# Sparse expert weights by indexed accumulating DMAs instead of one-hot products; expert tiles turned two ahead

## The reference, cut to what matters

```python
def block(xb):                                   # 128 tokens
    q = (xb @ w_q).reshape(t, 8, 2, 128)
    s = einsum('thpd,hpkd->thpk', q, sub_keys)   # 8 heads, 2 key sets of 128
    sv, si = top_k(s, 16)
    cand = sv[:, :, 0, :, None] + sv[:, :, 1, None, :]
    cv, ci = top_k(cand.reshape(t, 8, 256), 16)  # 16 experts of 16384 for each token and head
    idx = i1 * 128 + i2;  g = softmax(cv)
    act = gelu(einsum('thkd,td->thk', expert_down[idx], xb))
    return einsum('thk,thkd->td', g * act, expert_up[idx])
```

## Time and profile before

| | |
|---|---|
| median of 3 runs | 4651.68 us (4647.34 to 4653.0) |
| the profiled execution | 4650.75 us |
| its span, first to last instruction | 4649.0 us |
| mean granted TensorE clock | 0.969 |
| busy: TensorE matmul / VectorE / ScalarE / GpSimd | 92% / 56% / 29% / 31% |
| moved by DMA | 838.99 MB, 180 GB/s mean |
| `queries` | about 1600 to 1876 us |
| `experts_down` | 1876 to 3385 us |
| `experts_up` | 3385 us to the end |

### The profile page before, as it was taken

One profiled execution on the slowest core, in us unless ns is written; L12 is line 12 of the kernel. 1 busy time (PEld: TensorE's weight loads), 2 busy tenths in 40 slices (PEclk: granted clock), 3 DMA queues, 4 the chain that ended last, 5 costly groups with the idle time before them and its releaser, 6 DMA issues. The chain is left out here.

```text
span 4649.0 us, 69126 instructions
## 1 busy us (share of the span) xinstructions
PE 4286.5 (92%) x22902; PEld 3639.0 (78%) x22933; DVE 2599.5 (56%) x5422; ACT 1341.0 (29%) x2021; POOL 1432.2 (31%) x1022
## 2 busy tenths in 40 slices
PE   8999999897997799799999999999979999999998
PEld 3788877686776689798999999999957777777776
DVE  3555211255665333677889898897644444444444
ACT  1132433344222421233333333333221111111112
POOL 0333333354334021222111111111144444444442
PEclk9999999899998899899999999999989999999999
DMA  7222233344562422555566665666587777777776
GB/s 272 56 95 95 99 104 98 93 118 118 165 195 90 152 64 63 177 198 197 173 215 218 204 207 198 219 215 210 199 270 245 248 246 249 246 250 248 251 248 213
DMA packets 632585, 838.99 MB, mean 180 GB/s; under 512 B 227732, under 2 KB 448164, under 8 KB 632484
## 3 DMA queue, kind: packets, MB, share of 16 engines
q1 hardware_dynamic: 514468, 476.96, 32.5%
q0 software_dynamic: 73728, 268.47, 17.3%
q10 hardware_dynamic: 44288, 92.29, 5.1%
HBM read 674.03 MB, written 163.58 MB: 180 GB/s over the span
## 5 line engine op out<-in xcount | busy, mean ns | idle before, releaser
L1874 PE MATMUL p_u<-h2T_hi,downT_hi 128*128 128x384 f32 x2048 | 715.0, 349 | 103.4 <-DVE downT_lo L1979 85.3
L1874 PE MATMUL p_u<-h2T_hi,downT_lo 128*128 128x384 f32 x2048 | 693.9, 339 | 0.0
L1874 PE MATMUL p_u<-h2T_lo,downT_hi 128*128 128x384 f32 x2048 | 692.8, 338 | 0.0
L1852 POOL DMA_INDIRECT down_rows<-in_peer_down_dram,row_ids x256 | 262.4, 1025 | 1264.4 <-DVE row_dots L2002 1187.8
L2381 PE MATMUL p_y<-up_hi,coef_hi 128*128 128x512 f32 x1488 | 587.2, 395 | 0.0
L2381 PE MATMUL p_y<-up_lo,coef_hi 128*128 128x512 f32 x1488 | 580.4, 390 | 0.0
L2381 PE MATMUL p_y<-up_hi,coef_lo 128*128 128x512 f32 x1488 | 579.4, 389 | 0.0
L2282 DVE TENSOR_TENSOR y_acc<-p_y,y_acc 128x512 f32<-128x512 f32 x372 | 256.4, 690 | 540.5 <-PE p_y L2381 540.5
L1874 PEld LDWEIGHTS p_u<-h2T_hi,downT_hi 128*128 128x128 f32 x2048 | 391.3, 191 | 116.4 <-issue 116.4
L2178 POOL TENSOR_TENSOR up_lo<-up_raw,up_hi 128x1024 fp32r<-128x1024 f32 x128 | 323.0, 2524 | 419.8 <-ACT up_hi L2212 418.7
L508 PE MATMUL p<-hT_hi,w_hi 128*128 128x512 f32 x1024 | 405.0, 396 | 0.0
(11 more groups left out here) (343 smaller groups left out, 7888.8 us busy)
## 6 DMA issues: line engine op xcount, KB each, us to landing
down_raw<-in_peer_down_dram SPq DMA_DIRECT2D x128, 512.0 KB, 4.4
up_raw<-in_peer_up_dram SPq DMA_DIRECT2D x128, 512.0 KB, 5.3
scratch_gu<-gelu_out ACTq DMA_DIRECT2D x128, 384.0 KB, 2.3
gelu_in<-scratch_gu SPq DMA_DIRECT2D x128, 384.0 KB, 4.1
weights_in<-scratch_w SPq DMA_DIRECT2D x128, 384.0 KB, 6.4
w_raw<-in_w_in_dram SPq DMA_DIRECT2D x64, 512.0 KB, 4.0
w_ada_sb<-in_w_ada_dram SPq DMA_DIRECT2D x12, 2048.0 KB, 15.4
scratch_w<-weights_out SPq DMA_DIRECT2D x48, 512.0 KB, 3.7
```

Of the source, the lines that this page charges most:

```text
L1852: pool.indirect_dma_start(out=rows[:, n % ROWS, :], out_offset=None, in_=inp["peer_down"][0], in_offset=bass.IndirectOffsetOnAxis(ap=row_i ...
L1874: mm = pe.matmul(ps_u[u][half][:, 0:HD], d[:, u, k, :], h2[h][:, k, half * HD:(half + 1) * HD], start=(n == 0), stop=(n == 3 * KD - 1))
```

## The change

Four things, all for the expert layer.

1. The weight matrix is not built from one-hot products any more. `scratch_w` is now `[128 expert tiles, 128, 768 tokens]` and is set to zero during `project_in`, with 64 DMAs of two expert tiles each from a zeroed SBUF tile. Then, for each head of a dense block, the 16 picks of 128 tokens are sent with 16 indirect DMAs that add (`compute_op=ALU.add`): each writes 128 single floats, one for a token, at the offset expert x 768 + token, which VectorE makes as `sent_ids`. A head's sends wait until the last send of the head before has landed. Five heads of the first dense block are selected and sent in `queries`, the other 43 in `experts_down`. The one-hot operations on VectorE, their products on TensorE, ScalarE's copies and SP's stores of weights are gone.
2. `experts_down` has 51 selections (8 for fetched block 1, 43 dense), spread over the first 60 of 64 steps by `head_of`, the fetched ones taking turns with the first dense ones. Row gathers have a ring of 14 buffers and are issued two steps ahead; dot products go straight to `row_u`.
3. Expert tiles are turned two ahead: two PSUM buffers `p5_down`, four buffers each of `down_raw`, `downT_hi`, `downT_lo` and `gelu_out`.
4. `experts_up` reads `weights_in` in runs of 3072 bytes and waits for no weight store; `row_spread` has four buffers and is made a group ahead; the quads stand after slots 4 and 8, and two of them in the first group, after which the other groups have one pair each. Most hardware loops are written out.

The core of the diff:

```diff
+SENT = 4
+EARLY = 5
+RING = 14
...
# project_in, SP
                         sp.dma_start(w_raw[:, u], w_in(col, i)).then_inc(w_loaded[u], 16)
+                        if isinstance(i, int) and i == 0:
+                            sp.wait_ge(zero_set, 1)
+                        sp.dma_start(scratch["w"][bass.ds(i * CLEAR, CLEAR)].rearrange("e p t -> p e t"),
+                                     zero[:].unsqueeze(1).to_broadcast([P, CLEAR, TD])).then_inc(w_cleared, 16)
...
+def select_end(dve, b, step, exp_done, n, id_f, ids, scale, weight, chosen):
+    dve.wait_ge(step, n * SEL_STEPS + 24)
+    dve.scalar_tensor_tensor(id_f, b["pick"][:, 0], float(PK), b["pick"][:, 1], ALU.mult, ALU.add).then_inc(step, 1)
     dve.wait_ge(exp_done, n + 1)
     dve.reciprocal(b["inv"][:], b["exp_sum"][:]).then_inc(step, 1)
...
+        dve.tensor_scalar(ids, id_f, float(TD), scale, ALU.mult, ALU.add).then_inc(step, 1)
+    dve.wait_ge(step, n * SEL_STEPS + 26)
+    dve.tensor_scalar(weight, b["exp"][:], b["inv"][:], None, ALU.mult).then_inc(chosen, 1)
+def send_weights(pool, b, w_flat, sent, chosen, k, part):
+    r, half = k % SENT, TOPK // 2
+    if part == 0:
+        pool.wait_ge(chosen, k + 1)
+        if k:
+            pool.wait_ge(sent[(k - 1) % SENT], 16 * TOPK * ((k - 1) // SENT + 1))
+    for j in range(part * half, part * half + half):
+        pool.indirect_dma_start(out=w_flat, out_offset=bass.IndirectOffsetOnAxis(ap=b["sent_ids"][:, r, j:j + 1], axis=0),
+                                in_=b["sent_g"][:, r, j:j + 1], in_offset=None, compute_op=ALU.add
+                                ).then_inc(sent[r], 16)
...
# queries, GpSimd: after the cut of tile n
+                    if n >= 5 and (n - 5) // 2 < EARLY:
+                        send_weights(pool, sel, w_flat, sent, weights_chosen, (n - 5) // 2, (n - 5) % 2)
...
# experts_down
+        fetched = [(a, h) for a in range(1, NA) for h in range(PH)]
+        dense = [(NA, h) for h in range(EARLY, PH)] + [(b, h) for b in range(NA + 1, TB) for h in range(PH)]
+        heads = [x for pair in zip(dense, fetched) for x in pair] + dense[len(fetched):]
+        LAST = STEPS - 4
+        def head_of(s):
+            n = (s + 1) * len(heads) // LAST
+            return n - 1 if s < LAST and n > s * len(heads) // LAST else None
...
# GpSimd
+                for c in range(2 * FETCH):
+                    fetch(c)
+                for s in range(STEPS + 2):
+                    for c in range((s + 2) * FETCH, min((s + 3) * FETCH, TA)):
+                        fetch(c)
+                    if s >= 2 and head_of(s - 2) is not None and heads[head_of(s - 2)] in dense:
+                        for part in range(2):
+                            send_weights(pool, sel, w_flat, sent, weights_chosen, k, part)
+                        k += 1
...
# TensorE
-                def weights(ws, pair):
...
+                def four(p, last):
+                    for i in range(4):
+                        products(p, i, 0)
+                        if not last or i < 2:
+                            turn(p, i + 2)
+                        products(p, i, 1)
...
# VectorE
-                def hits(hh, r, ws, b):
...
+                for s in range(STEPS):
+                    head, before = head_of(s), None if s == 0 else head_of(s - 1)
+                    if 2 * s + 2 < E1:
+                        low(2 * s + 2)
+                    if before is not None:
+                        choose(before)
+                    for c in range(s * FETCH, s * FETCH + FETCH // 2):
+                        dot(c)
+                    if head is not None:
+                        dve.wait_ge(s_loaded[head % 2], 16 * (head // 2 + 1))
+                        select_keys(dve, sel, step, head)
+                    if 2 * s + 3 < E1:
+                        low(2 * s + 3)
+                    for c in range(s * FETCH + FETCH // 2, (s + 1) * FETCH):
+                        dot(c)
+                    if head is not None:
+                        select_picks(dve, sel, step, iota, head)
...
# experts_up: SP
-                        sp.dma_start(w[:, u].rearrange("p (h t) -> p h t", t=WT),
-                                     scratch["w"][:, :, bass.ds(n, 1), :].rearrange("h p o t -> p (h o) t")
-                                     ).then_inc(w_loaded[u], 16)
+                    sp.dma_start(w[:, u], scratch["w"][n]).then_inc(w_loaded[u], 16)
...
# GpSimd: gathers of a quad wait for the quad before
+                    if n >= SETS:
+                        pool.wait_ge(quad_done, n - SETS + 1)
...
+                for g in range(1, GROUPS):
+                    n = (g - 1) * NA + SETS
                     cut(g, 0)
+                    fetch(n)
                     cut(g, 1)
                     cut(g, 2)
+                    if NA > 2:
+                        fetch(n + 1)
                     cut(g, 3)
+                    fetch(n + NA - 1)
...
# VectorE
+                    for q in range(NA):
+                        spread_rows(g * NA + q)
...
# TensorE: first group, then the others
+                            elif j < NA:
+                                quad(j)
...
-                        if s == 0:
-                            quad(g * 2 - 1, 1)
-                        if s == SLOTS // 2:
-                            quad(g * 2, 0)
+                        for q in range(NA):
+                            if s == (q + 1) * SLOTS // (NA + 1):
+                                quad(g * NA + q)
```

More of the change, by code:

```diff
@@ L1771, in experts_down @@
+        rows_loaded = [m.sem(f"down_rows_loaded{i}") for i in range(RING)]
+        dot_done = m.sem("row_dot_done")
         down = inp["peer_down"][0].rearrange("(e p) d -> e p d", p=P)
[L1772 to L1784 removed]
@@ L1840, in _, with load, load_scores @@
-                for hh in range(2):
-                    sp.wait_ge(w_stored[hh], 16 * (PIECES * (ND - hh) + 1))
-                    sp.wait_ge(gu_stored[hh], 16 * (E1 // 2 + 1))
+                def load(n):
+                    if n >= 4:
+                        sp.wait_ge(turned, n - 3)
+                    sp.dma_start(raw[:, n % 4], down[n]).then_inc(loaded[n % 4], 16)
+                def load_scores(n):
+                    b, h = heads[n]
+                    if n >= 2:
+                        sp.wait_ge(step, (n - 2) * SEL_STEPS + SCORES_READ)
+                    sp.dma_start(sel["scores"][:, n % 2], scratch["scores"][b * PH + h]).then_inc(s_loaded[n % 2], 16)
@@ L1844, in _ @@
+                load(0)
+                load(1)
+                load(2)
+                load(3)
+                for s in range(STEPS):
+                    for n in (2 * s + 4, 2 * s + 5):
+                        if n < E1:
+                            load(n)
+                    if s + 1 < STEPS and head_of(s + 1) is not None:
+                        load_scores(head_of(s + 1))
+                for r in range(4):
+                    sp.wait_ge(gu_stored[r], 16 * (E1 // 4))
             @block.gpsimd
@@ L1856, in _, with turn @@
+                assert k == len(dense)
+                for r in range(SENT):
+                    pool.wait_ge(sent[r], 16 * TOPK * len(range(r, k, SENT)))
             @block.tensor
             def _(pe):
-                ahead(pe, *turned, *w_mm)
-                def turn(s, u):
-                    pe.wait_ge(loaded[u], s * 16 + 16)
+                ahead(pe, *gelu_done[0], *gelu_done[1])
+                def turn(p, i):
+                    pe.wait_ge(loaded[i % 4], (p + i // 4) * 16 + 16)
@@ new lines, in store @@
+                def store(n):
+                    for half in range(2):
+                        act.wait_ge(gelu_done[n % 2][half], n // 2 + 2)
+                    act.dma_start(scratch["gu"][n], gu[:, n % 4]).then_inc(gu_stored[n % 4], 16)
+                cut(0)
+                cut(1)
+                for n in range(E1):
+                    gelu(n, 0)
+                    if n + 2 < E1:
+                        cut(n + 2)
+                    if n % 2 == 0 and n and head_of(n // 2 - 1) is not None:
+                        select_act(act, sel, step, exp_done, head_of(n // 2 - 1))
+                    gelu(n, 1)
+                    store(n)
```

736 lines of the change are left out of this document (283 added, 453 removed).

## The result

The changed kernel takes 4873.28 us (median of 4 runs, 4870.31 to 4874.19), beside 4651.18 for the kernel before (4 runs): 1.048 times as long (95% interval 1.046 to 1.050). The forecast was 4489 us, the range 4400 to 4700. The profiled execution has a span of 4868.6 us, 219.6 more than before.

What follows compares the result with a forecast made beforehand. GpSimd's issues of sends and gathers were to bound `experts_down`, TensorE being relieved. 4650.75 - 153 (`experts_down`) + 3 (`queries`) - 13 (`experts_up`) = 4488, median 4489 us; range 4400 to 4700.

Steps and rivals of the forecast that it cites:

- The price of a send: GpSimd in `experts_down`: 1.34 us an issue, taken from the row gathers; stage 1359 us against 1512, -153 us.
- The first rival: GpSimd in `experts_down`: sending dearer than gathering; break-even 1.6 us a send, 4968 us in all at 2.10; chance 0.12.
- the 377: Start of `experts_down`: first 377 us, until VectorE has done step 19, in which GpSimd keeps up with the sends.
- TensorE's side: `experts_down`: one-hot passes and the 1.8 us wait go, leaving 64 x 18.4 = 1178 us.
- VectorE: `experts_down`: some 16 of 18.4 us a step, hidden with little room; five more selections in `queries` hidden too.
- The dots' 0.10 us an issue: `experts_down`: VectorE's two-input operations hold GpSimd's issues by 1.7 us over 17.6 issues, 0.10 each.
- The DMA engines fill up: Rival, `experts_down`: 88,064 one-float packets bind from 110 ns each; at 0.175 us 4852 us in all; chance 0.07.
- The wait at each head: GpSimd's sends: each head waits for the landing of the head before, covered by four gathers between; 0.
- Clearing: Projection: 64 zeroing stores, 50 MB, behind weight loads; 0, at most under 5 us without cover.
- `experts_up`: Stage after `experts_down`: spreads -39, late quads +28, first group +8, start -10, last quad -4; sum -13 us.
- The first group's stall: `experts_up`, first group: quad 1 comes 18 products after quad 0 with 12.3 us to go for its rows; +8 us.
- the late gathers: `experts_up`: second quad's rows, asked for only after the first quad, land late; 31 x 0.9 = +28 us (16 to 41).

Runs made afterwards that it cites:

- 8 sends: Changed kernel with only 8 of the 16 picks of each head sent, the others left out: 4290.1 us, 0.923 of the kernel before.

## Why the prediction was wrong

**The price of a send: the step that failed.** The forecast took "1.34 us, between 1.24 and a bound of 1.42", from the gathers, with the argument that "a gather lists 128 addresses from 128 indices just the same". For writing alone that is right: x is 1.37. The adding is a second cost on GpSimd, 0.60 us an issue, that no row of before could show; with it x is 1.97. The first rival named place and mechanism, and its own sum holds with the measured price: 377 + 560 x 1.97 + 220 + 12 = 1712 us for 1734.8, and 9(8 x 1.97 - 10.4) = 48 us in `queries` for 44.7. The missing 23 us are in the 377 in which GpSimd was taken to keep up: the formula puts 220 issues (128 sends, 92 gathers) into them, and the trace has 203 (115 and 88) by then. 13 x 1.97 + 4 x 1.32 = 31 us of work were thus left over. The rival's break-even was 1.6. A chance of 0.12 for it was too small: the nearest rows bounded a different operation, and `compute_op` was the one word of the new instruction that no old one had.

**TensorE's side: right.** 64 x 18.4 = 1178 us was forecast, 18.6 a step is measured once GpSimd lets it (8 sends). In the changed kernel the 531 us between 1203.5 and 1734.8 hold 405 us of waits for `downT_lo` and products at the lower clock after them (TensorE is busy for 1258 us from 1917 to 3652, in the kernel with 8 sends for 1188).

**VectorE: right.** It never was the bound; it waits for rows (553 us) and for the landing of sends (103 us), both behind GpSimd's queue. The dots' 0.10 us an issue was right too.

**The DMA engines fill up: wrong, as forecast.** The share is 0.56 to 0.59 in the saturated part. In `queries`, where this queue carries only sends, the kernel after and, in the second fence, the one that writes without adding show (packets, MB, share):

```profile
q0 software_dynamic: 11376, 0.05, 19.1%
```

```profile
q0 software_dynamic: 2681, 0.51, 1.8%
```

The first is over 182 us: 0.191 x 16 x 182 / 11376 = 0.049 us a packet and 142 packets a send, close to the cheap end of 0.047 that the rival began from and far from the 0.110 at which it would have begun to bind. The second window (184 us) also holds one gather of rows.

**The wait at each head: 0, right.** Of 43 such waits none shows; the 9.1 us put down to landings are gaps of 0.3 us at gathers. The Trainium skill (DMA: Bandwidth & Descriptors, Rules for kernel authors) says that an accumulating DMA must be kept apart by a semaphore from another one on the same bytes, since one of the additions would be lost. Two heads of one token block can pick the same expert for a token, so between them the wait can't go; no run here shows the loss, and the traces show that the wait is free.

**Clearing: 0, right.** The projection's windows are the same, and in the kernel with 8 sends, which clears as much, `experts_down` begins 0.7 us earlier than before.

**`experts_up`: right sign, size off.** -13 was forecast, -47.5 came. A group fell from 38.2 to 36.9 us, which is the spreads' 31 x 1.26 = 39. The first group's stall is there, smaller than the 8 us: in the chain that ended last of the kernel after, its second quad starts at 3694.21, 10.0 us after the first has ended, and TensorE waits 3.6 us of them for the rows. From the stage's first load to the steady part it is 59.6 us (3652.0 to 3711.6) for 61.5, where the forecast had +8 - 10 = -2. Without the late gathers its own terms give -39 + 8 - 10 - 4 = -45. The term that was mis-sized is "31 x 0.9 = +28" for them; it measured 0. The landing of 8.3 us belongs to the old order of loads and gathers. In the kernel before with the new `experts_up`, the last of four gathers is issued here, and the four land in

```profile
3942.62 0.94 POOL L2153 DMA_INDIRECT up_rows<-in_peer_up_dram,row_ids_turned  x1 [0.30 <-issue]
```

```profile
DMA to landing us min/median/max: 5.8/5.8/5.8
```

that is at 3948.4, 1.3 us ahead of the quad at 3949.71. The median over all gathers of rows is 6.4 us there and 7.8 in the kernel before. That the quads moved against the tile loads is the likely reason; it was not tried by itself. The trace of the kernel after records no landings, and has the same gap of 11.15 us between its quads; in the kernel that writes without adding, which has the same `experts_up`, the median is 5.9 us.

**The sum.** +200 and +48 from the rival's formula in place of -153 and +3, and -47 in place of -13, would have given 4650.75 + 200 + 48 - 47 = 4852 us. The profiled execution took 4870.31: 23 us more in `experts_down`, as above, and 3 less in `queries`.

## What to carry to other kernels

When a new instruction differs from the nearest one in the trace by an option, the option is an unknown cost of its own: work out at what price the change breaks even and weigh that price before the chance. When work is moved from a wide engine to a queue that issues it piece by piece, count the pieces: 944 issues, 1.97 us for a send and 1.32 for a gather on average, decide this stage, whatever the arithmetic that they replace. And time the parts of a change by themselves: most of one of the four parts here was worth 44 us in the old kernel and was hidden behind the loss of another.

## What the runs showed of the hardware that was not expected

- An indexed DMA that adds costs GpSimd 1.55 us, one that writes floats 0.97, one that gathers floats or rows 0.94, each with 0.30 us to the next. The adding sends take this long from the first one on, with no other under way.
- A send that adds 128 floats leaves 142 to 144 packets, one that writes them 32: 184,320 and 98,304 packets on the queue, 73,728 of them of the 512 row gathers, the rest of 768 sends. The packets of an adding send took 0.049 us each.
- After a wait of 15.9 us TensorE's products start 0.32 us apart for 5 us, then 0.17. That is about half the pace, the lower of the clock's two levels (1.2 and 2.4 GHz); the granted clock of the window is 0.87, and 1.00 in windows without such waits.
- Gathers of the same rows had a median landing of 6.4 us in one order of loads and gathers and of 7.8 in another (5.8 and 8.3 for the two told of above).
